# Expert units of a two-layer encoder: low-part matmuls first, and the ring slot given back behind the fourth of them

## The chip, the cores and the metric
One core of one Trainium2 chip runs the whole program. Its engines are TensorE (PE, with its weight loads as PEld), VectorE (DVE), ScalarE (ACT), GpSimd (POOL) and SyncE (SP), which here issues the loads of the weights. The metric is the device time of one execution in microseconds, and lower is better. A profiled execution also gives the span from the first to the last instruction.

## The reference
256 tokens of 1024 channels pass two layers, all in float32. Layer 0 is a retention mixer and a dense SwiGLU; layer 1 is grouped-query attention and a mixture of experts. Each has adaLN shifts, scales and gates made from the vector c by products with the ada weights. The change touches the mixture of experts alone:

```
logits = h @ w_router + b_router;  top 2 of 8 experts, softmax over the two
for e in range(8):
    out += combine[..., e] * ((silu(h @ w_gate[e]) * (h @ w_up[e])) @ w_down[e])
```

w_gate and w_up are 8 x 1024 x 3584, w_down is 8 x 3584 x 1024: 352 MB of float32 weights, each read once.

## The kernel before, in words
**Split products.** Each float32 factor is split in two fp32r parts: high = the value rounded to fp32r, low = value - high. A product is the sum of three matmuls, high x high, high x low and low x high. The helper `three` (L2055 to L2059) issues them in this order: L2057 the activations' high part with the weights' high part, L2058 the activations' high part with the weights' low part, L2059 the activations' low part with the weights' high part. Activations are stationary (128 x 128), weights move (512 columns).

**Units and the ring.** Weights come in units of 128 x 2048 values, 1 MB, each loaded by two transfers of 512 KB. `stage` is a ring of RING = 6 slots. ScalarE's `high_e` (L1120) waits until a unit has landed and writes its high part to one of six buffers of its own (`hi_e`, L459: three slots of `hi`, and hi_m, hi_h, hi_r; unit b and unit b + 6 have the same one). VectorE's `low_e` (L1796) then subtracts and writes the low part in place: `lo` lies on the same memory as `stage`. TensorE's `unit_e` (L2468) waits for the low part, uses the unit in 12 matmuls, and the last of them increments `w_used`. SyncE's `load` (L487) of unit b waits for `w_used` >= b + 1, where the count starts at 6: so until unit b - 6 has been used up. That wait guards the slot of the ring, and by it also ScalarE's buffer of high parts, since ScalarE can touch unit b only once it has landed.

**Stages.** An expert is worked in seven chunks of 512 hidden columns. A chunk has six units: two of w_gate and two of w_up (`e_half`, L2538; 4 row tiles each), and two of w_down of the chunk before (`e_down_step`, L2503; 2 row tiles of 1024 columns, in two halves of 512). The order on TensorE is gate and up of chunk n (bank 0 and 1), down of chunk n - 1 (banks 4 and 5), and the four transposes of the activated chunk n (`e_turn`, L2497, instruction at L2500). ScalarE does four high parts, the copy `eaT_hi` of the transposes (L1164), two high parts and the silu (L1160); VectorE a low part, the product `eact` (L1854), three low parts, `eaT_lo` (L1863) and two low parts. All queues are in order. The first expert is special: `first_half` (L2547) takes the very first unit in two passes, the eight matmuls with the activations' high part (L2551, L2552) and then, behind a wait for `hg_lo`, the four with their low part (L2555). During the first expert VectorE also forms the adaLN products of layer 1's last parts (L1648), and TensorE sums them (L2028). Experts after the first gather their token rows by GpSimd (L733) and turn them on TensorE (L2494). The last two units are used by `e_down_last` (L2516), which gives no slot back. Once per expert ScalarE waits for index matmuls (L2478, copy L1155). At the end GpSimd reads the result rows back and combines them (L755 to L759), started by thresholds of `w_used`. Behind the routing it also writes zeros to these rows, 2 MB in two transfers.

**Code that the change touches:**

Of the kernel before, what the change touches and what calls it, by code (L numbers as in the profile page):

```python
# [35 lines left out]
RING = 6  # L36
# [77 lines left out]
def encoder(nc, x, l0_ada_w, l0_ada_b, l0_norm2_g, l0_ret_w_in, l0_ret_decay_logit,  # L114
# [5 lines left out]
    with ctx:  # L120
# [276 lines left out]
        put_tr = sem("put_tr")  # L397
        put_done = sem("put_done")
# [73 lines left out]
        def _(sp):  # L472
# [121 lines left out]
            def load_gate_up(e, b, col, more):  # L594
                for m, wv in ((0, mg_v), (2, mu_v)):
                    for g in range(2):
                        load(b + m + g, wv[e, :, 4 * g:4 * g + 4, col] if isinstance(e, int) else
                             wv[bass.ds(e, 1), :, 4 * g:4 * g + 4, col].rearrange("a p k n -> p (a k) n"), more)

            def load_down(e, b, kt, more):  # L600
                for g in range(2):
                    ks = bass.ds(kt + 2 * g, 2)
                    load(b + g, md_v[e, :, ks, :] if isinstance(e, int) else
                         md_v[bass.ds(e, 1), :, ks, :].rearrange("a p k n -> p (a k) n"), more)
# [7 lines left out]
            load_gate_up(0, U_MOE, slice(0, ECH), 0)  # L612
            for half in range(2):
                load_ada(A_AT, half, l1_ada_w, l1_ada_b, (A_AT - A_L1) * AC)
            chunks(0, 0, 1, 4)
# [147 lines left out]
        def _(act):  # L763
# [356 lines left out]
            def high_e(b, more=0, occ=0):  # L1120

                act.wait_ge(w_load[b % RING], 32 * (b // RING + 1) + occ * 32)
                nc.scalar.copy(hi_e(b), stage[:, b % RING, :]).then_inc(hi_done, 1)  # L1123
# [897 lines left out]
        def _(pe):  # L2021
# [474 lines left out]

            def e_turn(n):  # L2497
                pe.wait_ge(e_act, n + 1)
                for k in range(4):
                    ins = nc.tensor.transpose(bank[:, 2, k * P:(k + 1) * P], eact[:, k * P:(k + 1) * P], ident)  # L2500
                ins.then_inc(e_tr, 1)

            def e_down_step(b, more, n, first, last, hi_a=eaT_hi, lo_a=eaT_lo, between=None):  # L2503
                pe.wait_ge(e_lo, n + 1)
                for g in range(2):
                    h, l = unit_e(b + g, 2, more)
                    for c2 in range(2):
                        for k in range(2):
                            cols = slice(c2 * CB, (c2 + 1) * CB)
                            ins = three(bank[:, 4 + c2, :], hi_a[:, 2 * g + k, :], lo_a[:, 2 * g + k, :], h[:, k, cols],  # L2510
                                        l[:, k, cols], first and g == 0 and k == 0, last and g == 1 and k == 1)
# [26 lines left out]
            def e_half(b, j, more):  # L2538

                for g in range(2):  # L2540
                    h, l = unit_e(b + 2 * j + g, 4, more)
                    for k in range(4):
                        ins = three(bank[:, j, :], hg_hi[:, 4 * g + k, :], hg_lo[:, 4 * g + k, :], h[:, k, :], l[:, k, :],
                                    g == 0 and k == 0, g == 1 and k == 3)
                    ins.then_inc(w_used, 1)

            def first_half():  # L2547

                h, l = unit_e(U_MOE, 4, 0)
                for k in range(4):  # L2550
                    mm(bank[:, 0, :], hg_hi[:, k, :], h[:, k, :], start=(k == 0), stop=False)  # L2551
                    mm(bank[:, 0, :], hg_hi[:, k, :], l[:, k, :], start=False, stop=False)  # L2552
# [5 lines left out]
                for k in range(4):  # L2558
                    ins = three(bank[:, 0, :], hg_hi[:, 4 + k, :], hg_lo[:, 4 + k, :], h[:, k, :], l[:, k, :], False, k == 3)
# [94 lines left out]
```

## Time and profile before
| | us |
|---|---|
| median of 3 runs (lowest, highest) | 1547.91 (1545.68, 1550.44) |
| the profiled execution | 1543.31 |
| its span | 1541.4 |
| TensorE busy | 1493.5 |
| VectorE busy | 1341.0 |
| ScalarE busy | 990.3 |

The times of the rows are of the profiled execution and count from the start of its span. A matmul of 512 columns is shown with 0.39 us but starts 0.23 us after the one before, since they are pipelined: the distance of the starts is its cost. PEclk is the granted TensorE clock, 1.00 for 2.4 GHz and 0.50 for 1.2 GHz. The DMA share is the mean busy share of the 16 DMA engines. "Idle before" in brackets names what ended the idle time.

### The profile page before, as it was taken

How to read it: one execution, taken by the hardware profiler on the slowest of the kernel's cores; microseconds unless marked ns; L12 is line 12 of the kernel's file. 1: busy time of each engine (PE TensorE's matmuls, PEld its weight loads, DVE VectorE, ACT ScalarE, POOL GpSimd, SP SyncE). 2: the span in 40 equal slices, each digit the busy share in tenths (PEclk: the TensorE clock that was granted, in tenths of full speed). 3: DMA queues.
4: the chain of work that ended last, by engine and by line, in shares of the span. 5: the costliest groups of instructions: out<-in, count | busy, mean ns of one | idle time of the engine just before them, and what ended most of it. 6: DMA issues, size and time to landing. Idle time of an engine off the chain costs nothing.

```text
span 1541.4 us, 20466 instructions
## 1 busy us (share of the span) xinstructions
PE 1493.5 (97%) x6787; PEld 1222.1 (79%) x6787; DVE 1341.0 (87%) x1080; ACT 990.3 (64%) x826; POOL 206.0 (13%) x188
## 2 busy tenths in 40 slices
PE   7999998999998999999999999999999999999997
PEld 6777676788877787778888888888888888888785
DVE  6899888888889679998998988888988988888898
ACT  4554444444447556677777777777777777777674
POOL 0499800000030011001001001001001000000320
PEclk9999999999999979999999999999999999999999
DMA  9989836998975379999999999999999999999993
GB/s 340 390 303 351 298 99 216 313 311 303 300 250 177 121 264 367 391 334 381 389 366 376 388 369 375 385 367 373 390 367 374 390 363 367 388 377 362 391 393 140
DMA packets 238897, 508.71 MB, mean 330 GB/s; under 512 B 15494, under 2 KB 38150, under 8 KB 238728
## 3 DMA queue, kind: packets, MB, share of 16 engines
q1 hardware_dynamic: 233824, 491.52, 87.6%
q0 software_dynamic: 4448, 14.55, 2.7%
q10 hardware_dynamic: 584, 2.11, 0.3%
q8 instruction: 24, 0.39, 0.1%
q14 instruction: 17, 0.14, 0.0%
HBM read 502.12 MB, written 7.87 MB: 331 GB/s over the span
## 4 chain that ended last, share of the span: by engine, by line
PE 80%; DVE 10%; DMA 3%; issue 2%; ACT 2%; SPq 1%; ACTq 0%; DVEq 0%
PE bank L2057 24%; PE bank L2059 24%; PE bank L2058 24%; DMA stage<-in_l_moe_w_up 2%; DVE lo L1799 2%; PE bank L2500 1%; DVE lo L1265 1%; DMA stage<-in_l_ret_w_in 1%; DVE ada_acc L1648 1%; DVE ada_acc L1283 1%; PE bank L2164 1%; SPq L512 1%; PE bank L2028 1%; DVE hs L1353 1%; ACT hi L1123 0%
## 5 line engine op out<-in xcount | busy, mean ns | idle before, releaser
L1799 DVE TENSOR_TENSOR lo<-stage,hi 128x2048 fp32r<-128x2048 f32 x168 | 388.2, 2318 | 37.8 <-ACT hi L1123 37.2
L1123 ACT CAST hi<-stage 128x2048 fp32r<-128x2048 f32 x168 | 321.4, 1915 | 103.2 <-DMA stage<-in_l_moe_w_up 85.7
L2058 PE MATMUL bank<-lo,hg_hi 128*128 128x512 f32 x892 | 347.5, 390 | 0.0
L776 ACT CAST hi<-stage 128x2048 fp32r<-128x2048 f32 x68 | 130.0, 1913 | 106.2 <-PE bank L2059 85.1
L2058 PEld LDWEIGHTS bank<-lo,hg_hi 128*128 128x128 f32 x892 | 167.7, 188 | 33.4
L1265 DVE TENSOR_TENSOR lo<-stage,hi 128x2048 fp32r<-128x2048 f32 x68 | 156.4, 2303 | 23.9 <-ACT hi L776 18.1
L1799 DVE TENSOR_TENSOR lo<-stage,hi_h 128x2048 fp32r<-128x2048 f32 x56 | 128.3, 2291 | 55.0 <-ACT hi_h L1123 55.0
L2057 PE MATMUL bank<-hi,hg_hi 128*128 128x512 f32 x448 | 174.6, 390 | 1.5 <-DVE lo L1799 1.5
L2058 PE MATMUL bank<-lo,eaT_hi 128*128 128x512 f32 x448 | 174.4, 389 | 0.0
L2059 PE MATMUL bank<-hi,hg_lo 128*128 128x512 f32 x448 | 174.3, 389 | 0.0
L2057 PE MATMUL bank<-hi,hT_hi 128*128 128x512 f32 x400 | 162.3, 406 | 2.3 <-DVE hT_lo L1328 2.1
L2058 PE MATMUL bank<-lo,hT_hi 128*128 128x512 f32 x416 | 163.1, 392 | 0.0
L2059 PE MATMUL bank<-hi,hT_lo 128*128 128x512 f32 x400 | 157.0, 392 | 0.0
L1123 ACT CAST hi_r<-stage 128x2048 fp32r<-128x2048 f32 x56 | 107.1, 1913 | 50.5 <-DMA stage<-in_l_moe_w_gate 48.7
L1799 DVE TENSOR_TENSOR lo<-stage,hi_r 128x2048 fp32r<-128x2048 f32 x56 | 128.0, 2285 | 6.5 <-ACT hi_r L1123 5.9
L1799 DVE TENSOR_TENSOR lo<-stage,hi_m 128x2048 fp32r<-128x2048 f32 x56 | 128.2, 2290 | 6.0 <-ACT hi_m L1123 4.7
L1123 ACT CAST hi_h<-stage 128x2048 fp32r<-128x2048 f32 x56 | 107.2, 1914 | 34.4 <-DMA stage<-in_l_moe_w_gate 32.8
L1123 ACT CAST hi_m<-stage 128x2048 fp32r<-128x2048 f32 x56 | 107.2, 1915 | 34.0 <-DMA stage<-in_l_moe_w_down 33.9
L1283 DVE SCALAR_TENSOR_TENSOR ada_acc<-ada_w,cact,ada_acc 128x512 f32<-128x512 f32 x147 | 118.7, 807 | 4.2
L739 POOL DMA_INDIRECT y_rows<-yout,sidx x7 | 10.4, 1481 | 760.8 <-ACT yout L1176 760.8
L2057 PEld LDWEIGHTS bank<-hi,hg_hi 128*128 128x128 f32 x448 | 84.1, 188 | 20.0 <-DVE lo L1799 2.4
L2058 PEld LDWEIGHTS bank<-lo,eaT_hi 128*128 128x128 f32 x448 | 84.1, 188 | 17.5 <-issue 0.5
(379 smaller groups left out, 2799.7 us busy)
## 6 DMA issues: line engine op xcount, KB each, us to landing
stage<-in_l_moe_w_gate SPq DMA_DIRECT2D x224, 512.0 KB, 5.0
stage<-in_l_moe_w_up SPq DMA_DIRECT2D x224, 512.0 KB, 5.4
stage<-in_l_moe_w_down SPq DMA_DIRECT2D x224, 512.0 KB, 5.1
ada_w<-in_l_ada_w SPq DMA_DIRECT2D x40, 1024.0 KB, 5.8
stage<-in_l_ret_w_in SPq DMA_DIRECT2D x48, 512.0 KB, 8.6
stage<-in_l_ffn_w_gate SPq DMA_DIRECT2D x22, 512.0 KB, 7.4
stage<-in_l_ffn_w_up SPq DMA_DIRECT2D x22, 512.0 KB, 8.4
stage<-in_l_ffn_w_down SPq DMA_DIRECT2D x22, 512.0 KB, 8.5
```

Of the source, the lines that this page charges most:

```text
L512: sp.dma_start(pre_w[half][:, k], src[:, :, half * HALF:(half + 1) * HALF]).then_inc(pre_load[half * KT + k], 16)
L776: nc.scalar.copy(hi_of(b), stage[:, b % RING, :]).then_inc(hi_done, 1)
L1123: nc.scalar.copy(hi_e(b), stage[:, b % RING, :]).then_inc(hi_done, 1)
L1265: nc.vector.tensor_tensor(lo[:, b % RING, :], stage[:, b % RING, :], hi_of(b).bitcast(F32), ALU.subtract).then_inc(lo_done, 1)
L1283: ins = nc.vector.scalar_tensor_tensor(out=acc, in0=ada_w[:, half, j, :], scalar=cact[:, k:k + 1], in1=acc if k else ada_b[:, :], op0=ALU. ...
L1353: ins = nc.vector.scalar_tensor_tensor(out=acc, in0=pre_w[half][:, k], scalar=cact[:, k:k + 1], in1=acc, op0=ALU.mult, op1=ALU.add)
L1648: ins = nc.vector.scalar_tensor_tensor(out=acc, in0=ada_w[:, half, k % AK, :], scalar=cact[:, k:k + 1], in1=acc if k else ada_b[:, :], op0 ...
L1799: nc.vector.tensor_tensor(lo[:, b % RING, :], stage[:, b % RING, :], hi_e(b).bitcast(F32), ALU.subtract).then_inc(lo_done, 1)
L2028: mm(bank[:, 3, :], ones, ada_acc[:, c % 2, :], start=True, stop=True).then_inc(a_sum, 1)
L2057: mm(dst_ap, a_hi, w_hi, start=first, stop=False)
L2058: mm(dst_ap, a_hi, w_lo, start=False, stop=False)
L2059: return mm(dst_ap, a_lo, w_hi, start=False, stop=last)
```

## The change
A new semaphore count `w_low` gives back the slot of the ring. It reuses `pre_load[0]`, which stands at 16 when the expert stage begins. In the units of the experts TensorE first issues the four matmuls with the weights' low part; the fourth increments `w_low`. Then come the eight with the weights' high part (helper `two`), and the last increments `w_used` as before. In `first_half` the first unit keeps its order and gets the increment behind its last low-part matmul. SyncE's loads of the expert units wait for `w_low`, except those whose slot was last used by the attention's output units, which wait for `w_used` as before (`old`). ScalarE's `high_e` gets a second wait, for `w_used` >= b + 1, because the load's wait no longer says that the buffer of high parts is free. The first chunk of SyncE's loop is written out before it; the order of the loads is the same.

```diff
+        w_low, w_low_from = pre_load[0], 16
...
+            def load_e(b, src, more, old):
+                if old:
+                    sp.wait_ge(w_used, b + more + 1)
+                else:
+                    sp.wait_ge(w_low, more + (w_low_from + b - RING - U_MOE + 1))
+                nk = src.shape[1]
+                dst_ap = stage[:, b % RING, :].rearrange("p (k n) -> p k n", k=nk)
+                for ks in (slice(0, nk // 2), slice(nk // 2, nk)):
+                    sp.dma_start(dst_ap[:, ks, :], src[:, ks, :]).then_inc(w_load[b % RING], 16)
...
-            load_gate_up(0, U_MOE, slice(0, ECH), 0)
+            load_gate_up(0, U_MOE, slice(0, ECH), 0, 4)
             for half in range(2):
                 load_ada(A_AT, half, l1_ada_w, l1_ada_b, (A_AT - A_L1) * AC)
-            chunks(0, 0, 1, 4)
+            load_gate_up(0, U_MOE + 4, slice(ECH, 2 * ECH), 0, 2)
+            load_down(0, U_MOE + 8, 0, 0)
+            chunks(0, 0, 2, 4)
...
             def high_e(b, more=0, occ=0):
                 act.wait_ge(w_load[b % RING], 32 * (b // RING + 1) + occ * 32)
+                act.wait_ge(w_used, b + 1 + more)
                 nc.scalar.copy(hi_e(b), stage[:, b % RING, :]).then_inc(hi_done, 1)
...
+            def two(dst_ap, a_hi, a_lo, w_hi, last):
+                mm(dst_ap, a_hi, w_hi, start=False, stop=False)
+                return mm(dst_ap, a_lo, w_hi, start=False, stop=last)
...
@@ e_down_step
-                    for c2 in range(2):
+                    halves = [slice(c2 * CB, (c2 + 1) * CB) for c2 in range(2)]
+                    for c2, cols in enumerate(halves):
                         for k in range(2):
-                            cols = slice(c2 * CB, (c2 + 1) * CB)
-                            ins = three(...)
+                            ins = mm(bank[:, 4 + c2, :], hi_a[:, 2 * g + k, :], l[:, k, cols], start=first and g == 0 and k == 0, stop=False)
+                    ins.then_inc(w_low, 1)
+                    for c2, cols in enumerate(halves):
+                        for k in range(2):
+                            ins = two(bank[:, 4 + c2, :], hi_a[:, 2 * g + k, :], lo_a[:, 2 * g + k, :], h[:, k, cols],
+                                      last and g == 1 and k == 1)
                     ins.then_inc(w_used, 1)
@@ e_half
                     for k in range(4):
-                        ins = three(...)
+                        ins = mm(bank[:, j, :], hg_hi[:, 4 * g + k, :], l[:, k, :], start=g == 0 and k == 0, stop=False)
+                    ins.then_inc(w_low, 1)
+                    for k in range(4):
+                        ins = two(bank[:, j, :], hg_hi[:, 4 * g + k, :], hg_lo[:, 4 * g + k, :], h[:, k, :], g == 1 and k == 3)
                     ins.then_inc(w_used, 1)
@@ first_half
-                    mm(bank[:, 0, :], hg_hi[:, k, :], l[:, k, :], start=False, stop=False)
+                    ins = mm(bank[:, 0, :], hg_hi[:, k, :], l[:, k, :], start=False, stop=False)
+                ins.then_inc(w_low, 1)
                 pe.wait_ge(hg_lo_done, 1)
```

## Rows read from the trace of the kernel before

**Rows 1.** Busy time by engine, and chain of waits, whole span.
```profile
PE 1493.5 (97%) x6787; PEld 1222.1 (79%) x6787; DVE 1341.0 (87%) x1080; ACT 990.3 (64%) x826; POOL 206.0 (13%) x188
PE 80%; DVE 10%; DMA 3%; issue 2%; ACT 2%; SPq 1%; ACTq 0%; DVEq 0%
```

**Rows 2.** Stretches; columns in the first line, busy time in us.
```profile
core 0: us, PE busy (x) PEld busy (x) DVE busy (x) ACT busy (x) POOL busy (x), PEclk, DMA share, GB/s
600.00:700.00 100.00, 96.34 (x427) 76.66 (x426) 93.45 (x64) 70.25 (x48) 0.00 (x0) 1.00 0.99 368
...
1000.00:1100.00 100.00, 100.00 (x460) 82.92 (x459) 87.32 (x50) 74.51 (x50) 4.87 (x6) 1.00 1.02 376
```

**Rows 3.** TensorE in order of time, steady stage: start, us, line, tiles.
```profile
1004.74 0.39 PE L2059 MATMUL bank<-hi,eaT_lo 128*128 128x512 f32 x1
1004.96 0.39 PE L2057 MATMUL bank<-hi_m,eaT_hi 128*128 128x512 f32 x1
...
1007.69 0.60 PE L2500 MATMUL bank<-cst,eact 128*128 128x128 f32 x4
1008.04 0.48 PE L2057 MATMUL bank<-hi_h,hg_hi 128*128 128x512 f32 x1
1008.36 0.40 PE L2058 MATMUL bank<-lo,hg_hi 128*128 128x512 f32 x1
...
1024.50 0.60 PE L2500 MATMUL bank<-cst,eact 128*128 128x128 f32 x4
```

**Rows 4.** Waits (total, times, longest) in 566:700, 1450:1500 and 700:1500.
```profile
PE bank L2500 <- DVE eact L1854: 2.2, 4, 0.7
PE bank L2028 <- DVE ada_acc L1648: 0.9, 1, 0.9
...
PE bank L2057 <- DVE lo L1799: 1.5, 2, 1.1
...
ACT ix L1155 <- PE bank L2478: 24.0, 7, 4.0
```

**Rows 5.** The first unit's release, in order of time.
```profile
565.22 1.36 PE L2555 MATMUL bank<-hi,hg_lo 128*128 128x512 f32 x4
...
566.61 0.89 SPq L493 DMA_DIRECT2D stage<-in_l_moe_w_up  x2
```

**Rows 6.** VectorE and ScalarE in order of time, steady stage.
```profile
1002.63 2.29 DVE L1799 TENSOR_TENSOR lo<-stage,hi_h 128x2048 fp32r<-128x2048 f32 x1 [0.37 <-ACT hi_h L1123]
...
1010.54 0.57 ACT L1164 CAST eaT_hi<-bank 128x512 fp32r<-128x512 f32 x1
```

**Rows 7.** TensorE in order of time, first expert, behind waits.
```profile
607.00 0.19 PEld L2057 LDWEIGHTS bank<-hi_m,eaT_hi 128*128 128x128 f32 x1 [0.43 <-DVE lo L1799]
...
610.59 0.66 PE L2500 MATMUL bank<-cst,eact 128*128 128x128 f32 x4 [0.58 <-DVE eact L1854]
...
659.37 1.13 PE L2028 MATMUL bank<-ada_acc,cst 128*128 128x512 f32 x2 [0.85 <-DVE ada_acc L1648]
```

**Rows 8.** VectorE in order of time, first expert, behind waits.
```profile
592.46 2.29 DVE L1799 TENSOR_TENSOR lo<-stage,hi_r 128x2048 fp32r<-128x2048 f32 x1 [1.74 <-ACT hi_r L1123]
...
643.17 2.29 DVE L1799 TENSOR_TENSOR lo<-stage,hi_h 128x2048 fp32r<-128x2048 f32 x1 [0.89 <-ACT hi_h L1123]
```

**Rows 9.** Stretches of 2 us, first expert, columns as in rows 2.
```profile
578.00:580.00 2.00, 2.00 (x11) 1.65 (x10) 1.71 (x9) 1.38 (x2) 0.36 (x3) 1.00 0.51 207
...
600.00:602.00 2.00, 2.00 (x11) 1.65 (x10) 1.97 (x4) 1.31 (x2) 0.00 (x0) 1.00 1.06 389
```

**Rows 10.** VectorE, GpSimd and TensorE in order of time, end.
```profile
1453.80 7.12 DVE L1799 TENSOR_TENSOR lo<-stage,hi 128x2048 fp32r<-128x2048 f32 x2 [0.43 <-ACT hi L1123]
...
1456.17 2.59 POOL L759 TENSOR_TENSOR moe<-moe,grow 128x1024 f32<-128x1024 f32 x1
...
1460.97 0.50 PE L2057 MATMUL bank<-hi,hg_hi 128*128 128x512 f32 x1 [1.14 <-DVE lo L1799]
```

**Rows 11.** The line of SyncE's loads, 700 to 1440.
```profile
DMA to landing us min/median/max: 3.6/5.1/8.4
```

More of the change, by code:

```diff
@@ L593, in _, with load_gate_up @@
                 load(U_AOUT + k, ao_v[:, 4 * kg:4 * kg + 4, n * CB:(n + 1) * CB])
-            def load_gate_up(e, b, col, more):
+            def load_e(b, src, more, old):
[7 more added lines that the diff above has]
+                    sp.dma_start(dst_ap[:, ks, :], src[:, ks, :]).then_inc(w_load[b % RING], 16)
+            def load_gate_up(e, b, col, more, old=0):
                 for m, wv in ((0, mg_v), (2, mu_v)):
                     for g in range(2):
-                        load(b + m + g, wv[e, :, 4 * g:4 * g + 4, col] if isinstance(e, int) else
-                             wv[bass.ds(e, 1), :, 4 * g:4 * g + 4, col].rearrange("a p k n -> p (a k) n"), more)
+                        load_e(b + m + g, wv[e, :, 4 * g:4 * g + 4, col] if isinstance(e, int) else
+                             wv[bass.ds(e, 1), :, 4 * g:4 * g + 4, col].rearrange("a p k n -> p (a k) n"), more, m + g < old)
             def load_down(e, b, kt, more):
@@ L602, in load_down @@
                     ks = bass.ds(kt + 2 * g, 2)
-                    load(b + g, md_v[e, :, ks, :] if isinstance(e, int) else
-                         md_v[bass.ds(e, 1), :, ks, :].rearrange("a p k n -> p (a k) n"), more)
+                    load_e(b + g, md_v[e, :, ks, :] if isinstance(e, int) else
+                           md_v[bass.ds(e, 1), :, ks, :].rearrange("a p k n -> p (a k) n"), more, False)
             def chunks(e, more, first, last):
@@ L2506, in e_down_step @@
                     h, l = unit_e(b + g, 2, more)
-                    for c2 in range(2):
+                    halves = [slice(c2 * CB, (c2 + 1) * CB) for c2 in range(2)]
+                    for c2, cols in enumerate(halves):
                         for k in range(2):
-                            cols = slice(c2 * CB, (c2 + 1) * CB)
-                            ins = three(bank[:, 4 + c2, :], hi_a[:, 2 * g + k, :], lo_a[:, 2 * g + k, :], h[:, k, cols],
-                                        l[:, k, cols], first and g == 0 and k == 0, last and g == 1 and k == 1)
+                            ins = mm(bank[:, 4 + c2, :], hi_a[:, 2 * g + k, :], l[:, k, cols], start=first and g == 0 and k == 0, stop=False)
[4 more added lines that the diff above has]
+                                      last and g == 1 and k == 1)
                     ins.then_inc(w_used, 1)
@@ L2558, in first_half @@
                 for k in range(4):
-                    ins = three(bank[:, 0, :], hg_hi[:, 4 + k, :], hg_lo[:, 4 + k, :], h[:, k, :], l[:, k, :], False, k == 3)
+                    ins = mm(bank[:, 0, :], hg_hi[:, 4 + k, :], l[:, k, :], start=False, stop=False)
+                ins.then_inc(w_low, 1)
+                for k in range(4):
+                    ins = two(bank[:, 0, :], hg_hi[:, 4 + k, :], hg_lo[:, 4 + k, :], h[:, k, :], k == 3)
                 ins.then_inc(w_used, 1)
```

2 lines of the change are left out of this document (removed).

## The prediction, made before the changed kernel was run
> **What bounds the kernel now.** I read the page's first part and the chain of waits first: TensorE is busy for 97% of the span and holds 80% of the chain [rows 1]. Then the busy time by stretch: in the expert stage, from 566 us to about 1530, TensorE shows no idle time at all in a stretch such as 1000 to 1100, at the full granted clock, while VectorE has 13% and ScalarE 25% to spare; from 600 to 700 it lacks 3.7 us [rows 2]. TensorE in order of time says what its pace is: matmuls of 512 columns start 0.227 us apart, across a unit's end as within it (1004.74 to 1004.96), and one chunk of six units repeats from transposes to transposes in 1024.50 - 1007.69 = 16.81 us [rows 3]. That is the work itself: 72 x 0.227 = 16.3 plus about 0.5 for the transposes. No earlier load can shorten it.
>
> So the change can only win where TensorE waits. The list of its waits has 2.2 us for eact (four times) and 0.9 us for ada_acc in 566 to 700, and 1.5 us for low parts in 1450 to 1500 (twice) [rows 4]. Between them, some 750 us are back to back.
>
> **The release that moves.** A ring slot now comes back at the unit's fourth matmul and not at its twelfth: 8 x 0.227 = 1.81 us sooner. For the very first unit it is less: its four low-part matmuls are through when L2555 starts at 565.22 or a little later, the four of L2555 take 1.36 us, and the load is issued at 566.61 [rows 5]. That is 1.2 us (1.36 by the row, less the drain). In the steady stage each load simply lands 1.8 us sooner against TensorE, and this buys nothing at once: there the low part of a unit is ready at 1002.63 + 2.29 = 1004.92 and TensorE takes it up at 1008.04, 3.1 us later [rows 3, 6]. The margin becomes some 4.9 us. Its worth is what it absorbs.
>
> **Term 1, the first expert (566 to 700).** VectorE carries the adaLN products here besides the low parts. It is busy for 93.45 of 100 us there, the most of any stretch of the stage [rows 2]. TensorE waits four times for eact, first at 610.59 for 0.58 us, and once for ada_acc, 0.85 us at 659.37 [rows 4, 7]: 2.2 + 0.9 = 3.1 us. A matmul behind a wait takes longer to come out, 0.50 us at 1460.97 instead of 0.39 [rows 3, 10]; I count 0.16 for each of the five restarts, 0.8 in all, and 0.2 each for two weight loads held back, like that at 607.00 [rows 7]. Ceiling: 3.1 + 0.8 + 0.4 = 4.3 us.
> How much of it goes? This row of stalls is the debt of a VectorE that has more work than a chunk's time; its queue is in order, so it can only be served earlier, by the idle time that it had before: 1.74 us at 592.46, for a high part that had waited for its transfer [rows 8]. The transfers are at their limit behind that (share 1.06 and 389 GB/s in 600 to 602) but were not before: 578 to 580 ran at half load, while the queue waited for a slot [rows 9]. All landings behind these gaps shift by what the gaps give, between 1.2 (first unit) and 1.8 us (every later one). VectorE can take up to its 1.74. I take 1.6 us. Lower bound 0: the 2 MB zeroing of the y rows, on GpSimd's queue, need not shift and could take the gap. Upper bound 4.3, all stalls.
>
> **Term 2, the end (1450 to 1500).** The final combination's GpSimd operations lie beside the low parts. Two low parts take 7.12 us at 1453.80, where two take 2 x 2.29 = 4.6 [rows 6], because a GpSimd addition of 2.59 us starts at 1456.17, and TensorE then waits 1.14 us [rows 10]. The second wait of the list is 1.5 - 1.1 = 0.4 us, for the other token tile's combination [rows 4]. With 0.16 each for the restart: 1.86 us. The Trainium skill has the rule: a VectorE instruction with two SBUF inputs and a GpSimd instruction that reads SBUF exclude each other for the whole instruction (SBUF — State Buffer, Who interferes with whom). By that rule, the trace agrees: the pair is longer by 2.5 us, one whole addition. A margin longer by 1.8 us covers the larger lack of 1.14. These transfers are triggered by TensorE's progress, so they keep their place beside it. I take 1.8 of the 1.86; bounds 0 (if the low part is caught by two GpSimd operations instead of one) and 1.86.
>
> **Terms at nothing.** (a) The order of the matmuls: same 12 per unit, same weight loads, same banks; the row of starts shows 0.227 for every pairing of high and low. (b) ScalarE's own wait for the unit's end, one more instruction for each unit and some register arithmetic in the loops: it can bind only if the data land sooner than 1.81 us after the slot was given back, and the fastest of the steady-stage loads takes 3.6 us from issue to landing [rows 11]. Behind that wait on ScalarE stand the next high parts, eaT_hi and the silu, and VectorE waits for those; if each cost 0.1 us, it would lie in ScalarE's 25% of idle time, before 3.1 us of margin. (c) The in-order queues: a ScalarE that is 1.8 us ahead must not run into the transposes. It copies eaT_hi at 1010.54, and they are through by 1007.69 + 0.60 = 1008.29 [rows 3, 6]: 1.8 us fit, just. (d) Once per expert ScalarE waits up to 4 us for the index matmuls [rows 4]; its lead is cut back there as before, and rebuilt within a chunk. (e) 334 more increments on TensorE. (336 units less the last two.) None of today's increments, one at each unit's end, is seen in the starts, so I take nothing. No row shows an increment in mid-unit; the nearest hiccup between two matmuls is the one behind the transposes, 1008.36 - 1008.04 = 0.32 us instead of 0.23 [rows 3], so the worst is 334 x 0.09 = 30 us. The Trainium skill has a price that speaks against the change: increments on matmuls serialize at 26.3 ns each in the tail (TensorE: Matmul & The Clock Gate, The cost: per-tile semaphore tail). If that lay in the stream, an estimate from the page would be 334 x 0.026 = 8.8 us; the trace does not agree, since a start behind an increment comes 0.22 us after the last one, like the others. (f) SyncE's queue keeps its order of loads; the splitting of its first chunk moves nothing, and its waits of one semaphore become waits of another.
>
> **Sum.** 1.6 + 1.8 = 3.4 us. The profiled execution took 1543.31 us (span 1541.4 and 1.9 around it); 1543.31 - 3.4 = 1539.9. The median shown, 1547.91, is 1.003 times the profiled time, so the forecast on its scale is 1547.91 x 1539.9 / 1543.31 = 1544.5 us, 0.22% less. What can be told from no change here is about 0.3%, 4.6 us, so the likeliest verdict is no difference.
>
> **Rivals.**
> - All stalls go, faster than forecast (21%): the deeper lead saves all of 4.3 + 1.9 = 6.2 us, because VectorE gets 2.7 us more lead in the first expert than I give it. For it: VectorE waits again for a late high part at 643.17, 0.89 us [rows 8]. Against: the transfers are saturated there [rows 9], and no earlier issue makes them faster. 1547.9 - 6.2 = 1541.7.
> - Only the end gains, or nothing does (16%): the zeroing of the y rows eats the first gap. 1547.9 - 1.8 = 1546.1, or 1547.9 if GpSimd's operations hit elsewhere.
> - Slower (7%): the increment in mid-unit costs TensorE its back-to-back start. Place: the fifth matmul of every unit; price, by the hiccup behind the transposes, 30 us, less the 3.4 gained: 1574.5. It outweighs the gain from 0.01 us a unit on, and shows as slower from 8.0 / 334 = 0.024 us. Against it stand the starts at the unit ends [rows 3].
> - The change does nothing it says, as ScalarE's wait restores the old order: 1547.9; the 3.6 us of (b) exclude it, and I give it no chance of its own.
>
> **How the numbers follow.** Forecast 56%, rivals 21, 16 and 7. The forecast's own range, with 1.5 us for the median of a few runs, is 1542 to 1547; to 8 in 10 it takes in most of the larger saving and the case of nothing: 1540.5 to 1549. Faster by over 0.3% (below 1543.3): the first rival, 0.21, and a tenth of the forecast's 0.56, by the noise of the median: 0.27. Slower by over 0.3% (above 1552.5): 0.07. Within: 0.66.
>
> **What the profile of the changed kernel would show.** Right: matmul starts still 0.227 apart, also behind the fourth of a unit, and a chunk of 16.81 us; the first slot's load issued near 565.4; the margin from a finished low part to its unit up from 3.1 to about 4.9 us; the wait for low parts near 1461 and 1495 gone though the pair beside the addition still takes 7.1 us; the waits for eact in the first expert down from 2.2 to about 1 us. Wrong: a chunk longer than 16.9 us (increments or order), ScalarE idle with TensorE as releaser at L1123's successor (its new wait binds), or the first expert's waits as long as now.

## The result, and the profile after

Six runs of the changed kernel had a median of 1534.32 us (1531.31 to 1540.45), six of the kernel before 1544.93: a ratio of 0.9949, 95% interval 0.9932 to 0.9966. That is 10.2 us below the forecast of 1544.5 and outside its range. The profiled execution took 1531.31 us, with a span of 1529.5.

The same two kernels were compared again, and this first comparison turned out to be the largest of three: 0.9978 and 0.9971 followed (below). Executions of one kernel lie up to 9 to 13 us apart (1531.31 to 1540.45; 1535.55 to 1548.93 of the kernel before in one comparison), and much of that goes with the mean clock that TensorE was granted over the run. A least-squares fit of time on kernel and mean granted clock over all executions of this study (those of the first comparison's kernel before have no clock and are left out) gives 1.06 us less per 0.001 of clock, with 1.7 us left over per run. At equal clock the changed kernel (30 runs) lies **5.3 us +- 0.7** below the kernel before (128 runs), 1537.4 against 1542.7 at a mean clock of 0.987: a ratio of 0.9966. I call such differences "at equal clock" from here on; they are fitted, all other numbers are measured. The interval behind +- is twice the standard error. Where a stall itself brings the clock down, this way of counting leaves that part of its cost out. The change makes the kernel faster, by a third of a per cent.

The page of the changed kernel, busy time and chain of waits, answers to [rows 1]:

```profile
PE 1485.1 (97%) x6787; PEld 1216.9 (80%) x6787; DVE 1339.0 (88%) x1080; ACT 991.6 (65%) x826; POOL 201.9 (13%) x188
PE 84%; DVE 8%; DMA 2%; ACT 2%; issue 2%; SPq 1%; ACTq 0%; DVEq 0%
```

VectorE has lost 2 points of the chain and TensorE has gained 4. The two stretches of [rows 2]:

```profile
600.00:700.00 100.00, 98.16 (x441) 79.44 (x440) 94.66 (x63) 72.27 (x50) 1.47 (x1) 1.00 1.01 375
1000.00:1100.00 100.00, 100.00 (x458) 82.92 (x457) 87.73 (x51) 74.34 (x50) 5.29 (x6) 1.00 1.01 376
```

In the first expert TensorE now lacks 1.8 us instead of 3.7. In the steady stage it was full before and is full now. TensorE there in order of time (answers to [rows 3]), and below it VectorE:

```profile
998.99 0.60 PE L2520 MATMUL bank<-cst,eact 128*128 128x128 f32 x4
999.34 1.18 PE L2567 MATMUL bank<-lo,hg_hi 128*128 128x512 f32 x4
1000.36 0.39 PE L2514 MATMUL bank<-hi_h,hg_hi 128*128 128x512 f32 x1
1000.59 0.39 PE L2515 MATMUL bank<-hi_h,hg_lo 128*128 128x512 f32 x1
...
1004.46 0.39 PE L2514 MATMUL bank<-hi_r,hg_hi 128*128 128x512 f32 x1
1004.69 0.39 PE L2515 MATMUL bank<-hi_r,hg_lo 128*128 128x512 f32 x1
1004.92 0.39 PE L2567 MATMUL bank<-lo,hg_hi 128*128 128x512 f32 x1
```

```profile
991.47 2.29 DVE L1814 TENSOR_TENSOR lo<-stage,hi_h 128x2048 fp32r<-128x2048 f32 x1 [0.44 <-ACT hi_h L1138]
```

L2567 is the four low-part matmuls, L2514 and L2515 the other eight. Behind the fourth matmul, which now increments, the stream simply goes on: from the start at 1000.36 to that at 1004.92 there are 20 matmuls in 4.56 us, 0.228 each, with one unit's end and one such place in mid-unit among them. The low part of this chunk's first gate unit is ready at 991.47 + 2.29 = 993.76 and used at 999.34: a margin of 5.6 us where there were 3.1 [rows 3, 6]. One chunk says little, since the margin swings within an expert: over the 45 chunks after the first expert it has a median of 3.3 and 3.6 us in the two profiles before and of 4.6 to 4.9 in the three after. In one chunk of each later expert it is 1.25 us before and 1.1 after: there ScalarE has just waited for the index matmuls, which come at TensorE's pace, and has lost its lead. Those seven waits add up to 24.0 us before and 35.0 after, as a ScalarE that is further ahead has to wait longer [rows 4].

### Where the time went

The transposes of the chunks (`e_turn`) cut the expert stage in 55 stretches. I summed their distances by part, for every profiled kernel. In us (the last stretch, 54 to 55, is 15.6 everywhere):

| profile | first expert, turns 0 to 5 | turns 5 to 50 | of it, excess over 16.81 at 7 expert boundaries | turns 50 to 54 | all 55 |
|---|---|---|---|---|---|
| before | 90.80 | 767.85 | 1.2 | 69.56 | 943.84 |
| the same, a second profile | 89.79 | 768.16 | 1.5 | 69.22 | 942.82 |
| changed | 88.01 | 766.66 | 0.0 | 67.33 | 937.64 |
| the same, a second and a third | 88.37, 88.03 | 766.69, 766.66 | 0.0 | 67.81, 67.65 | 938.50, 937.96 |

What lies behind the last transposes is 21.9 us in all of these. So the gain is made of **three** parts: 1.4 to 2.8 us in the first expert, 1.4 to 2.2 us at the end, and 1.2 to 1.5 us at the boundaries between experts, which the prediction had at nothing. The mean of the two profiles before is 943.3, of the three after 938.0: 5.3 us, the same as the fit over all runs.

The span of the first profile fell by 11.9 us, though. Of that 5.6 us lie ahead of the stage: the first transposes come at 569.97 instead of 575.57. The first chunk's gate and up units run there already, but it is the granted clock that makes the difference. The stretch 555 to 565 of the changed kernel's first profile, and of its second, in which the transposes come at 575.92:

```profile
555.00:565.00 10.00, 10.00 (x51) 8.49 (x51) 8.94 (x23) 7.63 (x6) 0.00 (x0) 1.00 0.66 225
```

```profile
555.00:565.00 10.00, 10.00 (x40) 9.23 (x40) 4.83 (x3) 5.60 (x4) 0.00 (x0) 0.50 0.22 88
```

PEclk is 1.00 in one and 0.50, 1.2 GHz, in the other, of one and the same kernel: this part of the first span's fall is not the change's.

### The profile page after: what moved, and what is told of

Same layout as the page of the kernel before. It is cut to its first block, busy times and chain, and to the rows that moved or that the text cites. A ratio compares the mean times of both kernels' runs of the same rounds, so it can differ in the third digit from the quotient of the medians.

```text
span 1529.5 us, 20773 instructions
## 1 busy us (share of the span) xinstructions
PE 1485.1 (97%) x6787; PEld 1216.9 (80%) x6787; DVE 1339.0 (88%) x1080; ACT 991.6 (65%) x826; POOL 201.9 (13%) x188
## 3 DMA queue, kind: packets, MB, share of 16 engines
q1 hardware_dynamic: 233824, 491.52, 88.4%
## 4 chain that ended last, share of the span: by engine, by line
PE 84%; DVE 8%; DMA 2%; ACT 2%; issue 2%; SPq 1%; ACTq 0%; DVEq 0%
PE bank L2514 19%; PE bank L2515 19%; PE bank L2567 13%; PE bank L2072 7%; PE bank L2073 7%; PE bank L2074 7%; PE bank L2530 6%; PE bank L2520 2%; DVE lo L1814 1%; DMA stage<-in_l_ret_w_in 1%; DVE lo L1280 1%; DMA stage<-in_l_moe_w_gate 1%; PE bank L2179 1%; DMA stage<-in_l_ffn_w_up 1%; DVE ada_acc L1663 1%
## 5 line engine op out<-in xcount | busy, mean ns | idle before, releaser
L2567 PE MATMUL bank<-lo,hg_hi 128*128 128x512 f32 x888 | 243.2, 396 | 0.0
L2567 PEld LDWEIGHTS bank<-lo,hg_hi 128*128 128x128 f32 x888 | 162.5, 188 | 30.9
L2514 PE MATMUL bank<-hi,hg_hi 128*128 128x512 f32 x448 | 174.3, 389 | 0.0
L2515 PE MATMUL bank<-hi,hg_lo 128*128 128x512 f32 x448 | 174.3, 389 | 0.0
L2530 PE MATMUL bank<-lo,eaT_hi 128*128 128x512 f32 x440 | 119.5, 393 | 0.0
L2514 PEld LDWEIGHTS bank<-hi,hg_hi 128*128 128x128 f32 x448 | 84.1, 188 | 17.5
L2515 PEld LDWEIGHTS bank<-hi,hg_lo 128*128 128x128 f32 x448 | 84.1, 188 | 17.5
```

The costliest lines, as they stand in the source:

```text
L2514: mm(dst_ap, a_hi, w_hi, start=False, stop=False)
L2515: return mm(dst_ap, a_lo, w_hi, start=False, stop=last)
L2530: ins = mm(bank[:, 4 + c2, :], hi_a[:, 2 * g + k, :], l[:, k, cols], start=first and g == 0 and k == 0, stop=False)
L2567: ins = mm(bank[:, j, :], hg_hi[:, 4 * g + k, :], l[:, k, :], start=g == 0 and k == 0, stop=False)
```

## The experiments

Each timed experiment has 12 runs of its own and shares 23 to 35 runs of the kernel before. An interval is some +-0.0016, about 2.5 us, so the tables of stretches carry more than the ratios.

### The change itself again

> The changed kernel once more, for a second profile and more times. Known: median 1534.3 against 1544.9, ratio 0.9949; profiled 1531.3 against 1543.3. In the two profiles 5.6 us of the 11.9 were there before the first transposes of the expert stage, where the kernel before ran 17.1 us at 1.2 GHz between 548 and 566 us and the changed one 3.4 us. Theory A (lead and luck): the change is worth the 6.2 us of stalls that it absorbs, and the low clock in the routing stage comes and goes without it; this profile may then show 17 us of low clock there, the ratio stays within 0.994 to 0.998. Theory B (routing): the change itself keeps the clock up there; the profile shows 3.4 us again and the ratio is 0.992 to 0.994. Both: no wait for low parts at the end, 2.8 us less in the first expert.

> The changed kernel once more, unchanged. Theory A (its gain is about 5 us at equal mean granted clock, the first comparison's 10.6 us held clock that fell well for it): ratio 0.9960 to 0.9980, and 4.3 to 6.1 us below the kernel before at equal clock. Theory B (the gain is the first comparison's 0.995 and the second comparison of 0.9978 was the unlucky one): 0.9940 to 0.9955.

Measured: 0.9978 (0.9962 to 0.9993) and 0.9971 (0.9954 to 0.9987). The first comparison's 0.9949 did not come back; its runs of the changed kernel had a mean clock of 0.9887 against 0.9872 in all 30 together, which accounts for 1.6 of the 3.1 us by which its median lies below 1537.4.

### The release taken back, the order kept

```diff
-                if old:
+                if True:          # every load waits for w_used, as before
                     sp.wait_ge(w_used, b + more + 1)
```

> The changed kernel, but every load of the expert units waits for the unit's end again, as before; the low-part matmuls still come first, TensorE still makes the 334 additional increments and ScalarE still has its own wait. Theory A (lead): all of the gain hangs on the earlier slot, so 1.000 +- 0.001 of the kernel before, and the waits for eact (2.2 us) and for low parts at the end (1.5 us) are back. Theory B (the clock in the routing stage is kept up by something else in the change): 0.997. Theory C (order of the matmuls makes TensorE faster): 0.995, with starts closer than 0.227 us. If increments or ScalarE's wait cost something, over 1.001.

Measured: 1.0015 (0.9994 to 1.0035), +1.9 us +- 1.0 at equal clock. In the profile the first expert takes 89.60, the end 69.49 and all 943.54 us: the stretches of the kernel before. The two waits for late low parts at the end are back:

```profile
PE bank L2567 <- DVE lo L1814: 1.5, 2, 1.1
```

The whole gain hangs on the earlier release. The matmul order, the 334 increments and ScalarE's wait bring nothing. Whether they cost something is open: the +1.9 us is clear of zero by its interval, and the version with the order alone, below, has +0.1.

### The release in the first expert alone, and in the later ones alone

```diff
-  ... m + g < old)                                    # and False, for w_down
+  ... m + g < old or not isinstance(e, int))          # and not isinstance(e, int): first_only
+  ... m + g < old or isinstance(e, int))              # and isinstance(e, int):     rest_only
```

> The changed kernel, but only the loads of the first expert use the earlier release; the loads of all later units wait for the unit's end. Theory A: keeps the 2.8 us of the first expert and loses the 3.4 of the later ones (0.8 near 1280, 1.6 near 1460, 0.7 near 1495, 0.3 elsewhere), so 0.998, and the waits for low parts at the end are back. Theory B: 0.995.

> The mirror: the first expert's loads wait for the unit's end, those of the seven later ones use the earlier release. Theory A: no wait for low parts at the end, the waits for eact in the first expert back at about 2.2 us; 3.4 us of 1545, so 0.998. If the two parts are independent, the gains of this one and of the mirror add up to that of the whole change. Theory B: 0.995.

Measured: 1.0005 (0.9984 to 1.0026) and 0.9985 (0.9968 to 1.0001); at equal clock -0.3 and -3.5 us, +-1.0 each, which is (before rounding) 2.2 and 5.3 below the version with the old release. Their sum, 7.5, is about the full change's distance to it, 7.2: against this version the parts add up. Against the kernel before they make 3.8 together, where the whole change makes 5.3; the intervals of +-1.0 each just allow that. The profiles say where. The first version's 600 to 700 reads like the changed kernel's:

```profile
600.00:700.00 100.00, 98.23 (x440) 79.70 (x440) 94.76 (x63) 71.87 (x48) 0.00 (x0) 1.00 1.00 372
```

but at one boundary it loses what it had won; TensorE, which had waited for nothing that the profile names:

```profile
804.93 1.19 PE L2567 MATMUL bank<-lo,hg_hi 128*128 128x512 f32 x4 [2.08 <-issue]
```

The other version has the old first expert (89.61), but 766.68 from turn 5 to 50 and 67.60 at the end. The later experts are worth more than the first, against my sum of nothing for all but the end. These two runs put me on the track of the boundaries.

### Two controls: the kernel before, and the order without ScalarE's wait and the increments

> The kernel before as an experiment of its own, for a second profile and for the spread of its times. Both theories: 1.000 +- 0.001 of itself. What it tells: whether the clock in the routing stage (17.1 us at 1.2 GHz in the first profile) comes and goes with the same code, and whether the first expert's 90.8 us from its first to its sixth group of transposes were usual. Theory A (luck): the low stretch may be 3.4 or 17 us. If the order of the matmuls is worth something in the first expert, this profile has 90.8 again against the 89.6 of the kernel with the new order and the old release; if not, about 89.6. From the first to the last transposes 943.5 +- 1.

Measured: 1.001 (0.9996 to 1.0024). That is what the comparison makes of no difference at all.

```diff
 # the kernel before, with the new order of matmuls, function load_e and written-out first chunk;
 # no w_low increment, no second wait in high_e, all loads wait for w_used
```

> The kernel before with the order of the matmuls alone: low-part matmuls first, but no increment in mid-unit, no second wait on ScalarE, and the loads wait for the unit's end. The kernel with the full change and the old release came out slower than before, 1.0015, and at the same mean clock by 2.4 us. Theory of the price in ScalarE's wait or the increments: this one is 1.000 of before. Theory of the order: 1.0015 again.

Measured: 0.9997 (0.9981 to 1.0014), +0.1 us +- 1.0 at equal clock. Order alone costs nothing that can be measured. The 1.8 us between this version and the one with the increments and ScalarE's wait, some +-1.4, are the most that anything here puts on these two together.

### ScalarE's second wait alone

```diff
             def high_e(b, more=0, occ=0):
                 act.wait_ge(w_load[b % RING], 32 * (b // RING + 1) + occ * 32)
+                act.wait_ge(w_used, b + 1 + more)
```

> The kernel before with nothing but ScalarE's second wait, for the end of unit b - 6, in front of each high part; the load's own wait already implies it, so it never holds ScalarE in fact. Theory of the price in ScalarE's wait (more instructions on its queue, less lead for VectorE): 1.001 to 1.0015, and each high part starts some 0.05 to 0.1 us later behind its data. If it is free: 1.000.

Measured: 0.9997 (0.9981 to 1.0013), +1.0 us +- 1.0 at equal clock. The added wait has a small price that the trace shows, as the first theory said: behind a landed unit the high part starts 0.02 us after the last landing in the kernel before and, for most units, 0.10 us after it here and in the changed kernel, so ScalarE loses some 0.07 us of its lead at a unit. Its profiled execution is the most instructive of all, with a span of 1548.4 us. A gate unit landed late at a boundary: ScalarE waited 2.44 us for it. ScalarE, then VectorE (the line numbers are one higher than before):

```profile
1156.79 1.91 ACT L1124 CAST hi_h<-stage 128x2048 fp32r<-128x2048 f32 x1 [2.44 <-DMA stage<-in_l_moe_w_gate]
1159.38 1.92 ACT L1124 CAST hi_r<-stage 128x2048 fp32r<-128x2048 f32 x1 [0.67 <-DMA stage<-in_l_moe_w_gate]
1161.20 1.01 ACT L1147 CAST hg_hi<-bank 128x1024 fp32r<-128x1024 f32 x1
```

```profile
1158.73 2.29 DVE L1800 TENSOR_TENSOR lo<-stage,hi_h 128x2048 fp32r<-128x2048 f32 x1 [2.55 <-ACT hi_h L1124]
1160.94 0.68 DVE L1855 TENSOR_TENSOR eact<-bank,esil 128x512 f32<-128x512 f32 x1
1161.55 2.28 DVE L1800 TENSOR_TENSOR lo<-stage,hi_r 128x2048 fp32r<-128x2048 f32 x1
1163.75 1.21 DVE L1859 TENSOR_TENSOR hg_lo<-bank,hg_hi 128x1024 fp32r<-128x1024 f32 x1
```

At an expert boundary the new expert's token rows have to be split too: `hg_lo`, their low part, stands on VectorE behind both gate low parts and `eact`. It is ready at 1163.75 + 1.21 = 1164.96, and TensorE starts at 1165.15 (a label "issue": no releaser was found for it, the time fits hg_lo):

```profile
1165.15 0.79 PE L2058 MATMUL bank<-hi_h,hg_hi 128*128 128x512 f32 x1 [2.70 <-issue]
...
1166.16 0.63 PE L2060 MATMUL bank<-hi_h,hg_lo 128*128 128x512 f32 x1
1166.59 0.63 PE L2058 MATMUL bank<-hi_h,hg_hi 128*128 128x512 f32 x1
```

The starts behind it are 0.43 us apart, not 0.23, and the stretches of 5 us show why:

```profile
1160.00:1165.00 5.00, 2.45 (x13) 1.81 (x11) 5.00 (x5) 4.31 (x4) 0.00 (x0) 0.95 1.03 397
1165.00:1170.00 5.00, 4.85 (x11) 3.79 (x12) 5.00 (x5) 4.17 (x4) 0.00 (x0) 0.50 0.37 145
1170.00:1175.00 5.00, 5.00 (x21) 4.03 (x20) 4.76 (x3) 2.34 (x2) 0.00 (x0) 0.87 0.58 186
```

TensorE had half a stretch without work, and behind it the granted clock was 0.50 (1.2 GHz). The boundary's excess is 5.8 us: 2.7 of waiting and 3.1 of slow clock. No wait of ScalarE for its new semaphore is seen here, so I do not lay this boundary to the added instruction: without it the same occurred with an excess of 2.7 (the kernel without the addition, below). That makes this run a single bad boundary, not a price of the wait.

### The rows' low part first, in the kernel before

This takes the boundary wait away without any change of the release.

```diff
@@ ScalarE, loop over the later experts
-                high_e(b + 1, m, o)
                 take_rows(w)          # hg_hi
+                high_e(b + 1, m, o)
@@ VectorE
-                low_e(b + 1, m)
                 low_rows(w)           # hg_lo
+                low_e(b + 1, m)
```

> The kernel before, with one thing moved at each of the seven expert boundaries: ScalarE copies the gathered rows' high part ahead of the second gate high part, and VectorE forms their low part (hg_lo) ahead of the second gate low part. Theory A (the late hg_lo is what costs at the boundaries): TensorE's waits for hg_lo there, 0.7 to 1.6 us per profile in all and single ones of up to 2.7 us, vanish or shrink by one gate low part and one gate multiplication, so the time goes down by 1 to 2 us, a ratio of 0.9985 to 0.9995, and first to last expert turn takes about 942 us against 942.8 and 943.8 of the kernel before. Theory B (the boundaries matter for nothing; the rest of the gain is elsewhere): ratio 1.000, 943 us.

Measured: 0.998 (0.9962 to 0.9998), -2.0 us +- 1.0 at equal clock; turns 5 to 50 take 766.66 us, exactly the changed kernel's, all seven boundaries have an excess of 0.01 or less, and all 55 stretches 941.59. Theory A holds. The seven other profiles that have the old release at the boundaries lose 1.2, 1.5, 2.0, 1.6, 7.3, 3.0 and 3.2 us there; the median is 2.0. The early release takes these waits away another way: the gate units land sooner, and hg_lo behind them is sooner too. Of the seven profiles with the early release at the boundaries six have no excess there; the one with wide matmuls (below) has 0.46 us at one boundary, so rare late ones are not excluded.

### How early: the release behind the eighth matmul

```diff
-                    ins.then_inc(w_low, 1)      # behind the 4th
...
+                        if k == 1:
+                            ins.then_inc(w_low, 1)      # behind the 8th; e_down_step: c2 == 0
```

> The changed kernel with the slot given back at the eighth matmul of a unit and not at the fourth: half the lead, 0.91 us. Theory A (the lead absorbs stalls): from the first to the last transposes between the 943.7 of the late release and the 938.1 of the early one, about 941 us; near 1460 a wait for low parts of 0.2 to 0.3 us (1.14 less 0.9), near 1495 none. Theory C (it is the order that counts, not the release): 938.

Measured, one execution: 1538.51 us, and all 55 stretches in 939.42 where 941 was expected. The boundaries are at 0.0, as with the full lead. The end is 68.09, 0.3 us above the longest with the full lead, and its wait for a low part is the second one (0.4 us), not the first as expected. The first expert is 89.03, between the two. In this profile half of the lead gets 3.9 of the 5.3 us.

### The final combination without its addition

GpSimd writes zeros to the second buffer in place of adding it; the sum of the two experts' rows is left out.

```diff
-  nc.gpsimd.tensor_tensor(moe[:, t, :], moe[:, t, :], ysec[t][:, :], ALU.add).then_inc(y_sum, 1)
+  nc.gpsimd.memset(ysec[t][:, :], 0.0).then_inc(y_sum, 1)
```

> The kernel before, but in the final combination GpSimd's addition of the two result rows is left out, and a clearing of the same size that only writes stands in its place; so the second expert's share is missing from the result. Theory of the shared read port (term 2): the two low parts beside it take 4.5 and not 7.1 us, both times; the waits for low parts near 1460 and 1495 are gone, and these two chunks take 16.8 and about 17.0 us instead of 18.0 and 17.7, without any more lead. If the low part is stretched by something else (the y rows' transfers, the clearing too), the pair stays at 7 us.

Measured, one execution: 1542.98 us. VectorE and GpSimd at the place of [rows 10]:

```profile
1453.86 4.98 DVE L1799 TENSOR_TENSOR lo<-stage,hi 128x2048 fp32r<-128x2048 f32 x2 [0.43 <-ACT hi L1123]
...
1456.22 0.96 POOL L759 MEMSET grow<- 128x1024 f32 x1
```

The pair takes 4.98 us instead of 7.12, and the chunk beside it 16.81 instead of 18.36; with the other token tile the chunk takes 17.06 instead of 17.61. So the addition makes those low parts late. By the Trainium skill (SBUF — State Buffer, Who interferes with whom) a GpSimd instruction that only writes does not get in the way of VectorE's second input. The trace agrees: with the other token tile the writing lies beside a low part, and that takes its usual 2.29 us.

```profile
1487.99 0.96 POOL L759 MEMSET normg<- 128x1024 f32 x1
...
1488.35 2.29 DVE L1799 TENSOR_TENSOR lo<-stage,hi 128x2048 fp32r<-128x2048 f32 x1
```

The whole time did not fall: this profile has a boundary with a wait of 2.47 us, 1.6 us of slow clock in the first chunk, and a new wait of 0.56 us for eact in the chunk between the two.

### Attempts at a version that beats both

```diff
@@ after_mul_first: VectorE, first expert, on the changed kernel
-            low_e(b + 1)
             e_mul(...)            # eact
+            low_e(b + 1)          # and the adaLN step moved behind the product
@@ routing_wide: TensorE ahead of the routing, on the changed kernel
-            keep_busy(4, 2)       # and keep_busy(9, 2)
+            wide_early(4)         # matmuls of 512 fp32r columns on finished data; the second 10
```

> The changed kernel, and in the first expert VectorE forms the product eact before the adaLN step (four chunks), and in the first chunk before the second low part. TensorE's waits for eact, 1.6 us and 3.2 us in the two profiles of the changed kernel, should go: 0.67 + 0.75 us sooner each. But if the first expert is bound by VectorE's sum of work, what is gained at eact comes back as a wait for a low part or for the adaLN sum. Theory of the queue's order: 1.5 us less than the changed kernel, 0.996 to 0.997 of before. Theory of the sum of work: no difference, 0.997 to 0.998.

> The changed kernel, and in the routing stage the idle-filling matmuls of TensorE (13, of 128 columns in float32, results unused) are replaced by 14 of 512 columns in fp32r, of about the same duration. Theory of the clock: the low stretch that begins near 548 us is 3.4 us or none in the profile, never 17; the times come closer together (the changed kernel's 12 runs span 7.5 us) and the median falls by 2 to 4 us, 0.995 to 0.996 of before. If the low stretch has nothing to do with what these matmuls do: 0.998, spread as before, low stretch 3.4 or 17 us.

> The changed kernel with both additions: the product eact before the adaLN step and before the second low part of the first chunk, and the idle-filling matmuls of the routing stage of 512 columns. Alone they gave 0.9972 and 0.9969 of before, where the change alone gave 0.9978 in 12 runs. If they are independent of it and of each other: 0.9965. If both differences were noise: 0.9975. At the same mean clock I expect 4.8 to 6 us less than before.

Measured: 0.9972 (0.9958 to 0.9987), 0.9969 (0.9955 to 0.9983) and, for both together, 0.9961 (0.9942 to 0.9979); at equal clock -5.4, -5.2 and -5.6 us, +-1.0, against the changed kernel's -5.3. None is better than the change by itself. The first moved the stall instead of removing it: in the first expert the waits for eact fell, and one for the adaLN sum took their place:

```profile
PE bank L2043 <- DVE ada_acc L1663: 0.7, 1, 0.7
PE bank L2509 <- issue: 0.5, 1, 0.5
PE bank L2520 <- DVE eact L1869: 0.5, 1, 0.5
```

Its first expert takes 89.48 us, more than the changed kernel's 88.0 to 88.4. The second has no slow clock from 511 to 575 us in its profile, as its theory wanted, but the first transposes come no sooner for it (575.35), TensorE waits 1.91 us for eact there, and 3.41 us of slow clock follow; its times still lie 8 us apart. What decides when the clock falls is open.

## Why the prediction was wrong

Its mechanisms were right, its sum put a term at nothing that is worth 2 us, and its scale stood on three runs.

**Order and increments at nothing: right.** The 334 increments cost nothing that a start shows, and the third rival's 30 us are excluded. The same stream with all of them and the old release runs 0.23 apart, and its 45 stretches take 768.82 less 1.99 at the boundaries = 766.83, 0.2 us above the changed kernel's.

**ScalarE's wait at nothing: it never binds, but it is not quite free.** Alone it is +1.0 +- 1.0 us. The list of ScalarE's waits from 700 to 1440 seems to show the sign of being wrong that I had named: high parts held by the unit's last matmul (L2515), 3 times in the first profile, 11 times in the second, where the longest is 1.8 us, and 6 times in the third. The label misleads. The longest, and the load that it needs:

```profile
876.54 3.61 SPq L604 DMA_DIRECT2D stage<-in_l_moe_w_up  x4
...
883.83 1.92 ACT L1138 CAST hi<-stage 128x2048 fp32r<-128x2048 f32 x1 [1.82 <-PE bank L2515]
```

The load is issued at 876.54, behind the fourth matmul of the unit whose slot it takes; that unit's last matmul starts at 877.93, and with its end the buffer of high parts is free. The second transfer lands at 883.73, 0.10 us before ScalarE starts. So ScalarE waited for the data, and a later unit's end happened to come beside the landing. In all of these waits of the three profiles the last landing lies 0.10 or 0.15 us before the start, as it does in nearly all of those that the list puts down to the DMA. That is the prediction's point (b): no load of 700 to 1440 lands sooner than 3.7 us after its issue. The second wait adds 0.07 us per unit behind the landing, less than the 0.1 us that (b) allowed for. I had covered that price by the "3.1 us of margin", and at the boundaries that cover does not exist.

**Term 1, the first expert, 1.6 us: right in size.** The first profile before takes 90.80, six others with the old release there 89.37 to 89.86 with a mean of 89.67; the changed kernel's three have a mean of 88.14. That is 1.5 us against the group. (The kernels without the addition, with the release in the first expert alone and with wide matmuls in the routing had 1.6 us of slow clock in their first chunk, 18.4 instead of 16.85: 91.03, 89.30 and 89.34. I leave them out here.) The mechanism is seen too: VectorE's idle time in the first expert (pauses of over 0.1 us, added up) is 3.3 to 4.5 us in the same seven profiles with the old release there and 2.1 to 2.4 in the changed kernel's three, and the 1.74 us before the low part of hi_r [rows 8] are gone. The release, in the second profile, at the clock of [rows 5]:

```profile
565.43 1.54 PE L2582 MATMUL bank<-hi,hg_lo 128*128 128x512 f32 x4
565.66 3.13 SPq L604 DMA_DIRECT2D stage<-in_l_moe_w_up  x4
```

The load is issued 0.23 us behind the start of the next matmuls, not 1.39 as in [rows 5]: 1.2 us sooner against TensorE's work, as worked out. In the first profile this unit ran at full clock, and the slot came back at 558.2. The waits for eact in 566 to 700 were forecast at about 1 us. They are 1.6 and 1.3 in the second and third profile, and 3.2 in the first, of which 1.92 lies at the very first transposes:

```profile
569.97 0.66 PE L2520 MATMUL bank<-cst,eact 128*128 128x128 f32 x4 [1.92 <-DVE eact L1869]
```

That wait is not the change's. TensorE comes to these transposes at full clock, and VectorE is not ready; the kernel without the addition, which has the old release, waits 1.88 us there.

**Term 2, the end, 1.8 us: right in mechanism and in size.** The pair beside the addition still takes its time, and no unit waits for it, answers to [rows 10]:

```profile
1441.91 7.01 DVE L1814 TENSOR_TENSOR lo<-stage,hi 128x2048 fp32r<-128x2048 f32 x2 [0.53 <-ACT hi L1138]
...
1444.19 2.58 POOL L773 TENSOR_TENSOR moe<-moe,grow 128x1024 f32<-128x1024 f32 x1
```

The two chunks with waits, 18.36 and 17.61 before, take 16.82 and 16.90: 2.2 us. That is the best of the three profiles. In the other two the first chunk is as short, but the second takes 17.41 and 17.25, with a wait of 0.23 us for a low part in one of them: this stall was not to be gone altogether. The four stretches are 67.3 to 67.8 in the three profiles after, and 68.9 to 69.6 in the seven others that have the old release there (the kernel without the addition aside): 1.6 us between the two means.

**"Between them, some 750 us are back to back": the step of the mechanism that failed.** I read this from windows of 100 us and from the list of waits. The list of before has a single 0.5 us for this stretch, without a releaser:

```profile
PE bank L2057 <- issue: 0.5, 1, 0.5
```

I passed over it, and over waits too short to be listed; adding up the distances of the transposes would have shown 1.2 us in seven places. The mean over executions is higher, since now and then one boundary costs 2 to 6 us, and such a one was not in the profile that I had. The term is about 2 us: -2.0 +- 1.0 by the kernel that removes it alone. With it the sum is 1.6 + 1.8 + 2.0 = 5.4, and 5.3 were measured at equal clock.

**The scale: the term that was mis-sized most.** "The forecast on its scale" took 1547.91, a median of three runs, for the level of the kernel before. Over 128 runs that level is 1542.7. So of the 10.2 us between forecast and result 5.2 are the level, 1.9 the missed term (5.3 less 3.4), and 3.1 the first comparison's changed runs, which lie below the 1537.4 of all 30: luck, half of it that of the clock (1.6 us). On the profiled execution's own scale the forecast was 1539.9, 2.5 us above 1537.4. The profiled execution of before, at 1543.31 next to three runs of up to 1550.44, said that the level was loose; I took it up to the median where I should have stayed between.

**The rivals.** "All stalls go" had the size nearly right (6.2 us) for a wrong reason: the first term went by 1.5 of its 4.3 us, and the rest came from the boundaries. "Only the end gains" is excluded by the first expert's 1.5 us and the boundaries' 2. The chance of "within 0.3%" was too high for a gain of 0.34%, which lies on the bound.

What is not shown: why some gate units land 2.4 us late just at a boundary. All 16 DMA engines are full there (share 1.03 above), the gathered rows travel at the same time, and no run separated the two.

## What to carry to other kernels

A slot that can be given back in the middle of its use should be, if the stream behind it has places where the consumer's margin is gone: here 1.8 us of lead, for 334 increments and one more wait of ScalarE per unit, took away the waits at the boundaries in six of seven profiles, the first stall at the end, and 1.5 us in the first expert; half of that lead got 3.9 of 5.3 us in one profile. Look for such places by the distance between equal marks of each period (here the transposes), not by busy shares or by the list of waits: a stall of 0.1 to 0.8 us seven times, with no named releaser, shows only there. A label in the list of waits names the semaphore that moved last, not the one that was missing: compare the landing before you believe it. And take the level of the kernel before from as many runs as there are; one profile and three runs differed by more than the change.

## What the runs showed of the hardware

- A single wait of TensorE can bring the clock down, and the same wait need not. One of 2.7 us in an otherwise full stream was followed by a granted clock of 0.50 (1.2 GHz); it cost 3.1 us more. Five profiles have a wait of 1.9 us at the first transposes of the stage: in three of them the clock was 0.50 for 3.4 us right behind it and the first chunk took 18.4 to 18.5 us, in two it stayed at 1.00 and the chunk took 16.86. A wait of 2.47 us in another place was not followed by it either: behind it the starts stayed at 0.23 us:

```profile
1400.96 0.49 PE L2057 MATMUL bank<-hi_h,hg_hi 128*128 128x512 f32 x1 [2.47 <-issue]
1401.29 0.40 PE L2058 MATMUL bank<-lo,hg_hi 128*128 128x512 f32 x1
1401.52 0.40 PE L2059 MATMUL bank<-hi_h,hg_lo 128*128 128x512 f32 x1
```

- Executions of the same kernel differ by when the clock is granted, by 6 us alone at the entry to the expert stage, where the first transposes come at 570 or at 576 us in profiles of one kernel.
- 334 increments in mid-stream do not show in the starts of the matmuls (0.2 us in 750, within what the profiles differ by). The whole time leaves room for up to 1.8 +- 1.4 us for them and ScalarE's second wait together.
- A second semaphore wait in front of a ScalarE instruction puts its start 0.10 us behind the landing of its data instead of 0.02.
